# Key pages, scores and sample sums one projection step sooner in a two-layer decoder step, with a fifth buffer for value pages

## What is computed

```python
gq, gk, gv, gg, glr, mu, mv, sq, sk, sv = split_cols(a @ w_in)    # 1024 -> 3088 columns
o_gla, s_gla = gla_mixer(gq, gk, gv, gg, glr, ...)                # gated linear attention, 4 heads
o_gm, v_gm = gmlp_mixer(mu, mv, ...)                              # spatial gating, 4 heads
# stick-breaking attention, 8 heads; the samples see 1024 past keys in 8 pages of 128 rows
z = einsum('bthd,bshd->bhts', q, k) * HEAD_DIM ** -0.5 + bias
log1m = where(mask, -softplus(z), 0.0)
suffix = cumsum(log1m, axis=3, reverse=True) - log1m
A = where(mask, exp(log_sigmoid(z) + suffix), 0.0)
o_sb = einsum('bhts,bshd->bthd', A, v)
o = concatenate([o_gla, o_gm, o_sb], -1) @ w_out
```

## Time and profile before

| | |
|---|---|
| runs of the kernel before | 1373.92, 1377.28, 1377.60 us; median 1377.28 |
| the profiled execution | 1376.02 us, span 1374.3 us |
| TensorE busy | 1319.7 us, 96% of the span; mean granted clock 0.991 |
| VectorE, ScalarE, GpSimd busy | 795.0, 585.0 and 81.6 us |
| moved | 324.59 MB, mean 236 GB/s |
| last input projection step ends (first layer) | 384.67 us |
| last `new_values` ends (first layer) | 443.43 us |

### The profile page before, as it was taken

The page is one execution under the profiler, slowest core; times in us unless marked ns, Lnnn a source line. Parts: engine busy times, 40 slices in busy tenths (PEclk is TensorE's granted clock), DMA queues, the critical chain, the costliest instruction groups (busy, mean ns, idle before and its releaser), DMA issues.

```text
span 1374.3 us, 34322 instructions
## 1 busy us (share of the span) xinstructions
PE 1319.7 (96%) x13994; PEld 1261.9 (92%) x13994; DVE 795.0 (58%) x1160; ACT 585.0 (43%) x963; POOL 81.6 (6%) x158
## 2 busy tenths in 40 slices
PE   6899999999989999999999999998998998999998
PEld 5899999999976899999989999998997787999998
DVE  2554554567895655555465555446788657555544
ACT  2533333443465543334453333345346555333343
POOL 4000000010041000000000000002003100000000
PEclk9899999999999999999999999999999999999999
DMA  9878789789989895568875566996998993565453
GB/s 329 252 229 270 214 249 307 220 257 325 313 269 355 259 325 153 154 168 277 269 237 154 161 174 199 293 269 192 334 336 251 331 325 106 160 175 155 138 168 98
DMA packets 424008, 324.59 MB, mean 236 GB/s; under 512 B 15655, under 2 KB 351911, under 8 KB 423888
## 3 DMA queue, kind: packets, MB, share of 16 engines
q1 hardware_dynamic: 421124, 317.03, 75.9%
q0 software_dynamic: 2464, 5.71, 1.3%
q10 hardware_dynamic: 300, 0.13, 0.0%
HBM read 318.03 MB, written 4.78 MB: 235 GB/s over the span
## 4 chain that ended last, share of the span: by engine, by line
PE 85%; DVE 4%; DMA 4%; SPq 2%; ACT 2%; issue 1%; DVEq 1%; POOL 0%; ACTq 0%
PE PS L601 23%; PE PS L602 23%; PE PS L603 23%; PE PS L627 4%; PE PS L885 2%; PE PS L655 2%; PE PS L656 1%; PE PS L657 1%; SPq L450 1%; PE PS L931 1%; DMA direct<-in_cache_sb_v 1%; DMA raw<-in_mix_w_out 1%; DMA raw<-in_ffn_w_in 1%; DVE w_lo L1684 1%; DVE direct L1959 1%
## 5 line engine op out<-in xcount | busy, mean ns | idle before, releaser
L1684 DVE TENSOR_TENSOR w_lo<-raw,w_hi 128x1024 fp32r<-128x1024 f32 (+1 forms) x368 | 392.9, 1106 | 443.8 <-ACT w_hi L1298 443.3
L1298 ACT ACTIVATE w_hi<-raw 128x1024 fp32r<-128x1024 f32 (+1 forms) x368 | 337.5, 960 | 651.5 <-PE PS L603 574.6
L601 PE MATMUL PS<-a_hi,w_hi 128*128 128x288 f32 x1760 | 524.0, 298 | 0.8 <-ACT ysq L1656 0.6
L602 PE MATMUL PS<-a_lo,w_hi 128*128 128x288 f32 x1760 | 519.2, 295 | 0.0
L603 PE MATMUL PS<-a_hi,w_lo 128*128 128x288 f32 x1760 | 517.6, 294 | 0.0
L601 PEld LDWEIGHTS PS<-a_hi,w_hi 128*128 128x128 f32 x1760 | 329.8, 187 | 4.7 <-issue 3.8
L603 PEld LDWEIGHTS PS<-a_hi,w_lo 128*128 128x128 f32 x1760 | 331.4, 188 | 0.0
L602 PEld LDWEIGHTS PS<-a_lo,w_hi 128*128 128x128 f32 x1760 | 330.4, 188 | 0.7 <-issue 0.4
L602 PE MATMUL PS<-h_lo,w_hi 128*128 128x288 f32 x704 | 208.4, 296 | 0.0
L601 PE MATMUL PS<-h_hi,w_hi 128*128 128x288 f32 x704 | 208.1, 296 | 0.0
L603 PE MATMUL PS<-h_hi,w_lo 128*128 128x288 f32 x704 | 208.0, 296 | 0.0
(11 more groups left out here) (321 smaller groups left out, 1134.6 us busy)
## 6 DMA issues: line engine op xcount, KB each, us to landing
raw<-in_ffn_w_in SPq DMA_DIRECT2D x176, 512.0 KB, 5.0
direct<-in_cond_w SPq DMA_DIRECT2D x240, 256.0 KB, 5.0
direct<-in_cache_sb_k SPq DMA_DIRECT2D x128, 256.0 KB, 4.6
direct<-in_cache_sb_v SPq DMA_DIRECT2D x128, 256.0 KB, 4.3
raw<-in_ffn_w_out SPq DMA_DIRECT2D x64, 384.0 KB, 3.7
raw<-in_mix_w_in SPq DMA_DIRECT2D x48, 512.0 KB, 7.4
raw<-in_ffn_w_out SPq DMA_DIRECT2D x64, 320.0 KB, 4.3
side<-in_cond_w SPq DMA_DIRECT2D x48, 256.0 KB, 5.3
```

The lines of the kernel that those rows point to most:

```text
L601: pe.matmul(out, whi, hi, start=begins and i == 0, stop=False)
L602: pe.matmul(out, whi, lo, start=False, stop=False)
L1298: act.activation(w_hi[:, s, at_:at_ + n], raw[:, s, at_:at_ + n], ACT.Copy)\
L1684: tt(w_lo[:, s, at_:at_ + n], raw[:, s, at_:at_ + n], w_hi[:, s, at_:at_ + n], ALU.subtract).then_inc(lo_done.sem, 1)
```

## The change

- Key chunks `2j-4` and `2j-3` follow step `j`, from 2 to 9. VectorE turns them at the end of its part of step `j-1`, behind the split; two queries are spread at step 2. SyncE interleaves key chunks with weights accordingly.
- The transpose of the query copies goes between the two halves of step 2, `part_offsets(0)` between those of step 10. The key rows (`rows_of(.., SK, ..)`) go behind step 10 and into step 11, `regroup(0)` directly behind step 11 with its result in banks 4 to 7.
- The sums of sample group 0 go from VectorE's step 10 to step 8, the offsets and weights to steps 10 and 11. The cap of group 1 moves from GpSimd to VectorE, its sums ahead of the prompt's masks. The gate's SiLU with its two table loads moves from ScalarE's step 11 to step 10.
- A fifth buffer, `extra`, takes value chunks 4, 9 and 14; the others rotate through `direct`. Value chunk 0 comes before the last two `prompt_scores`.
- On ScalarE `values_by_sample` and `prompt_log1p_exp(2)` go behind `weights_by_page(1)` and `sample_rows(0)`; `prompt_log1p_exp(0)` goes ahead of the first `gla_rows`. On TensorE `prompt_sums(1)` goes behind `regroup(1)`, which waits for `prompt_less(0)` alone.
- The weights of output steps 2 and 3 are issued ahead of the conditioning chunks. Tiles of the GLA state move, and the waits that this asks for are added.

```diff
-    KEYS_AT = {j: (2 * j - 6, 2 * j - 5) for j in range(3, 11)}
+    KEYS_AT = {j: (2 * j - 4, 2 * j - 3) for j in range(2, 10)}
...
+        extra = tile("extra", [P, 2048])
+        a_turn0 = tile("a_turn0", [P, 4 * NPG * 32], F32, at[0] - 8192)
...
+            def extra_chunk(l, n):
+
+                found = page_table_entries(4 * n)
+                if n < 5:
+                    sp.wait_ge(a_moved.sem, a_moved.at(l, 1))
+                else:
+                    sp.wait_ge(extra_used.sem, extra_used.at(l, n // 5))
...
-                mix_in(2, 3)
+                mix_in(2)
                 key_chunks(l, 0, 1)
+                mix_in(3)
+                key_chunks(l, 2, 3)
                 mix_in(4)
-                key_chunks(l, 2, 3)
-                mix_in(5)
                 for j in range(3, 9):
-                    mix_in(j + 3)
-                    key_chunks(l, *(n + 4 for n in KEYS_AT[j]))
+                    mix_in(j + 2)
+                    key_chunks(l, 2 * j - 2, 2 * j - 1)
+                mix_in(11)
                 for n in range(NPC):
-                    if n == 4:
+                    if n % 5 == 4:
+                        extra_chunk(l, n)
+                    else:
+                        page_chunk(l, cache_sb_v, DP_V, 4 * n, n - (n + 1) // 5)
+                    if n == 3:
                         for s in range(2):
                             mix(l, mix_w_out, POS_MO, s, s, s * 256)
-                    page_chunk(l, cache_sb_v, DP_V, 4 * n, n, n)
                 for s in range(2):
+                    mix(l, mix_w_out, POS_MO, 2 + s, s, (2 + s) * 256)
                     cond_seam(l, 0, 2 * s, 2 * s + 2)
-                    mix(l, mix_w_out, POS_MO, 2 + s, s, (2 + s) * 256)
...
+                            if (j, h) == (10, 0):
+                                pe.wait_ge(gate_x.sem, gate_x.at(l, 1))
+                                part_offsets(0, 7)
+                            if (j, h) == (11, 0):
+                                pe.wait_ge(z_got.sem, z_got.at(l, 5))
+                                rows_of(2, SK, 5, k_t)
...
+                    if j == 11:
+                        pe.wait_ge(off_added.sem, off_added.at(l, 1))
+                        pe.wait_ge(kv_k.sem, kv_k.at(l, 3))
+                        regroup(0)
...
+                pe.wait_ge(kv_v.sem, kv_v.at(l, 3))
+                turn_new(1)
                 pe.wait_ge(gm_y.sem, gm_y.at(l, 2))
-                prompt_sums(1, 2)
...
-                pe.wait_ge(c_sub.sem, c_sub.at(l, 2))
+                pe.wait_ge(c_sub.sem, c_sub.at(l, 1))
                 regroup(1)
                 new_values(0)
...
+                pe.wait_ge(a_copied.sem, a_copied.at(l, 2))
+                prompt_sums(1, 2)
+                value_chunk(8)
```

More of the change, by code:

```diff
@@ L473, in cond, with page_table_entries @@
                     cond_load(L - 1, c * D - D, slot)
-            def page_chunk(l, cache, dp, first, n, wait):
+            def page_table_entries(first):
                 _, found = nc.values_load_multi_w_load_instructions(
@@ L924, in value_chunk @@
                             pe.wait_ge(o_rows_got.sem, o_rows_got.at(l, g))
[L925 to L928, removed]
+                    d = n - (n + 1) // 5
+                    if n % 5 == 4:
+                        rows, done, by = extra[:, :], extra_used, 1
+                        pe.wait_ge(extra_in.sem, extra_in.at(l, n // 5 + 1) * 64)
+                    else:
+                        rows, done, by = direct[:, d % 4, :], direct_used, 1 if n < NPC - 1 else 4
+                        k = direct_in[d % 4]
+                        pe.wait_ge(k.sem, k.at(l, DP_V // 4 + 1 + d // 4) * 64)
+                    if n == NPC - 1:
+                        for slot in range(1, 4):
+                            pe.sem_inc(direct_in[slot].sem, 64)
                     for t in range(4):
@@ L932, in value_chunk @@
                                              a_keys[:, 4 * half + t, 32 * p:32 * p + 32],
-                                             direct[:, n % 4, 512 * t + p * P:512 * t + p * P + P],
+                                             rows[:, 512 * t + p * P:512 * t + p * P + P],
                                              start=v == 0 and t == 0, stop=False)
-                    last.then_inc(direct_used.sem, 1)
+                    last.then_inc(done.sem, by)
                 def new_values(g):
@@ L951, in turn_rows, with rows_of @@
                     last.then_inc(o_turned.sem, 1)
+                def rows_of(i, f0, bank, done):
+                    sl, n = token_tile(i)
+                    for p in range(PR):
+                        last = pe.transpose(PS[0:n, bank, p * P:p * P + P], Fm[:, f0 + p, sl], ident[:, :])
+                    last.then_inc(done.sem, 1)
                 for j in range(N_MI):
@@ L1048, in prompt_values @@
                     last.then_inc(op_sum.sem, 1)
-                def rows_of(i, f0, bank, done):
-                    sl, n = token_tile(i)
-                    for p in range(PR):
-                        last = pe.transpose(PS[0:n, bank, p * P:p * P + P], Fm[:, f0 + p, sl], ident[:, :])
-                    last.then_inc(done.sem, 1)
                 def gla_rows(i, bank):
@@ L1584, in sample_heads @@
                     last.then_inc(o_headed.sem, 1)
+                weights_by_page(0)
                 act.wait_ge(gate_b.sem, gate_b.at(l, 1))
@@ L1996, in turn_weights @@
                         dve.wait_ge(a_moved.sem, a_moved.at(l, g))
-                    dve.transpose(a_turn[:, :], z[:, g, 0:NZ]).then_inc(a_turned.sem, 1)
+                    else:
+                        dve.wait_ge(direct_used.sem, direct_used.at(l, DP_K + NPC))
+                    dve.transpose((a_turn if g else a_turn0)[:, :], z[:, g, 0:NZ]).then_inc(a_turned.sem, 1)
                 def spread_new(g):
@@ L2321, in _ @@
                 after(off_sum, l, 1)
-                pool.wait_ge(z_got.sem, z_got.at(l, 5))
-                new = z[:, 1, NZ:].rearrange("p (b t) -> p b t", t=TS)
-                pool.tensor_tensor(new, new, new_mask[:, :].unsqueeze(1).to_broadcast([P, 4, TS]), ALU.add)
-                pool.drain()
-                pool.tensor_scalar(sm[1][:, :], z[:, 1, :], TOP_Z, None, ALU.min).then_inc(ss_n.sem, 1)
                 pool.wait_ge(gate_e.sem, gate_e.at(l, 1))
```

206 lines of the change are left out of this document (113 added, 93 removed).

## The result

The change is slower, by a little: 1382.33 us median of 16 runs (1379.03 to 1384.78) against 1377.81 us (1373.72 to 1383.78), a ratio of 1.0032 with a 95% interval of 1.0020 to 1.0043. By the ratio that is 4.4 us, just over what this measurement can tell from no change. A second series of the same kernel gave 1.0039 (1.0022 to 1.0056). The prediction had said 1377.4 us and a range up to 1381.5: the time lies 0.8 us above it.

A forecast was written before the change was run, and what follows sets the result against it. TensorE, 96% busy, was taken as the bound: its own work plus waits. Per layer 0.7 + 0.3 us later, for two layers, less 0.6, gave +1.4 us on 1376.0, so 1377.4 us; range 1370.5 to 1381.5.

The forecast's parts named there:

- The query transpose waits 0.7 to 0.8 us: Between the halves of input step 2, TensorE newly waits 0.7 to 0.8 us for VectorE's query copy.
- Key waits go: In the input projection, TensorE's 0.3 us wait for key chunk 15 disappears.
- prompt_scores(2) waits 0.8, gla_rows(2) 1.7, regroup(1) at 417.0: Between input projection and regroup(1): new waits of 3.0 us in all, yet regroup(1) starts 2.9 us earlier.
- my walk: Hand-following of waits between queues through the first layer, using the earlier trace's instruction times; last input step ends at 387.2.
- Pages no longer bound: Value chunks' waits for pages vanish; chunk 15 is there at 436, six us before its use.
- From regroup(1) to prompt_sums(3) 15.4 us, waits 4.4: ScalarE's queue takes 15.4 us beside 11.0 of TensorE work; TensorE waits 4.4, and prompt_sums(3) starts 2.1 us later.
- The last `new_values` 0.7 us later: At the first layer's mixer end, the last new_values ends at 444.1 instead of 443.43.
- 0.7 + 0.3 - 0.6: Second layer's sum: new_values 0.7 us later, output products' a_lo wait 0.3, output step 3's weight wait 0.6 saved.
- Output step-3 weights earlier, -0.6: Second layer: weights issued ahead of two conditioning chunks save TensorE's 0.6 us wait; the chunks' delay costs nothing.
- my first paragraph: Claimed a change that only moves work can win no more than TensorE's waits: 13.4 us for both mixer layers.
- The rival of the table loads: Each ScalarE table switch costs a drain, 1.9 us more per layer: 1381.2 us; chance 0.05.

The follow-up runs named there:

- its second profile: The change run once more, unchanged, as a control: 1382.19 us (11 runs), 1.0039.
- the kernel with the FFN weights first: The change with the first FFN step's weights (slot 0) issued ahead of conditioning chunks 2 and 3: 1379.30 us, 1.0026.
- The kernel with the GLA copy moved: The change with FFN weights first, values_by_sample and pair 2's logarithm ahead of regroup(1), and ScalarE's first GLA copy ahead of pair 0's logarithm: 1373.31 us, 0.9971.
- the softplus kernel: The kernel with the GLA copy moved, plus pair 2's softplus ahead of the spread of new weights on VectorE: 1382.37 us, 1.0019.
- the five-edit kernel: The change with FFN weights, values_by_sample, pair 2's logarithm, first GLA copy and first mask all issued sooner: 1382.49 us, 1.0051.

## Why the prediction was wrong

Step by step, in the order of the prediction:

- *The query transpose waits 0.7 to 0.8 us*: 0.84. *Key waits go*: they did.
- *prompt_scores(2) waits 0.8, gla_rows(2) 1.7, regroup(1) at 417.0*: 1.5, 1.6, and 418.4. On the clock of before, the last input step ends at 387.0 (387.2 in my walk) and TensorE stands at `prompt_scores(2)` from 391.2 on, as in my walk. The copy that it needs was ready at 392.7 instead of 392.0. So `regroup(1)` comes 1.5 us earlier than before and not 2.9; the gain of this stretch was sized too high.
- *Pages no longer bound*: right, in every variant.
- *From regroup(1) to prompt_sums(3) 15.4 us, waits 4.4*: 16.7 us in the change's profile, with waits of 2.7 and half-clock work in the rest; 15.7 us in its second profile, where this stretch has the full clock, with waits of 4.5. Cause and size were right.
- *The last `new_values` 0.7 us later*: it ends 162.4 us behind the mixer's first product, against 159.3 before: 3.1 us later, and 162.3 in the second profile. How much of that is the clock's can be seen in the second layer of the kernel with the FFN weights first, a mixer at the full clock throughout: 161.0, against 159.3 and 160.0 in the two layers of before, 1.0 to 1.7 us later. In the same layer the mixer's column sums of `yacc` start 0.5 us later than in before's second layer, where my sum has 0.7 + 0.3 - 0.6 = 0.4. With the unforeseen wait mended and the clock full, the sum holds there.
- *Output step-3 weights earlier, -0.6, the conditioning chunks are used 20 us later, in the seam, and cost nothing*: **this step failed.** The 0.6 us came: no product step waits for `ysq` any more. But I asked only who uses the chunks that moved back, and not what is queued behind them on SyncE. There stand the FFN weights, and behind their split on VectorE the sum of squares that ends the mixer. Two runs put it at 2.5 us (each to about 1 us): one mends it in the change, the other makes it in before. With it the sum is +3.9 us; 4.4 were measured, and 2.8 (+-0.8) at the same clock.
- *The clock* has no term in the sum at all. I took the granted clock of the profiled execution (0.991) as given and costed waits at their own length. Nor are the waits all that a change can win or lose, as my first paragraph has it: before's profile holds 25 us of half clock. The change's runs have a clock lower by 0.0031 on average, and at 0.78 us for each 0.001 that goes with 2.4 us. At the same clock the change is 2.8 us slower than before; the two make the 5.2 us between the means of all runs.
- *The rival of the table loads*: the loads at 371.94 and 373.93 take 1.28 us each, and the SiLU between them starts 0.02 us behind the first. What followed the second started 0.73 us behind it, 0.03 us behind the operation of VectorE that it waited for. The Trainium skill ("ScalarE: Activation LUTs", What ACT_TABLE_LOAD costs) has a drain of about 1380 ns on top of each switch; the trace shows none here either.

So the result is on the slower side by two things: the wait that the sum put at nothing, which is settled, and the lower clock, which it left out and which goes with the rest. **What stays open** is why the change has a lower clock. It is not the swap on SyncE (0.9902 with it in before). It is not `values_by_sample` or the FFN weights (0.9857 with either mended, as the change's 0.9858). Whether the row of small products around `regroup(1)` has a part in it was not settled. The kernel with the GLA copy moved has 0.9876 and 46 us of TensorE waits in its profile, the one with the softplus moved as well 0.9811 and 44. The clock does not go by the sum of the waits, and a run's clock is an average over stretches that fall in other places each time; one profile for each kernel does not tell what decides.

## What to carry to other kernels

When a transfer is moved back in a queue because its data are used late, look at what stands behind it in that queue, and then at what stands behind that one's consumer on its engine: both queues are in order, and the loss came two steps from the move. An operation that costs nothing does so in one idle stretch; moved behind a hand-over it gets a price (4.8 us of copies in each layer, 3.9 us of time for both layers), and the group-1 sums show the same from the other side. When two profiles are laid over each other, take as zero the first instruction of the stretch in question. Counted from the seam ahead of the mixer, which has a half-clock stretch in before and none in the change, `regroup(1)` would seem to stand at 417.0. Where TensorE is 96% busy, compare kernels at the same granted clock before giving a difference of a few us to an edit.

## What was not expected of the hardware

**The clock.** TensorE's granted clock fell to half in stretches in which it was busy 10 us out of 10 by the profile, with no wait above 0.6 us in the 10 us before (the softplus kernel at 415). In the change it fell at 415 in one profile and at 400 in the next. Within a kernel, some runs at 0.981 took 8 to 9 us more than some at 0.988 (the kernel with the FFN weights first: 1386.3 us at 0.981 and 0.982, 1378.2 and 1377.1 at 0.988).

**VectorE beside GpSimd.** GpSimd's timeline in the five-edit kernel, and VectorE's scans there:

```profile
389.96 3.61 POOL L2383 TENSOR_TENSOR gt<-gt,Fm 128x576 f32<-128x576 f32 x2 [9.23 <-ACT gt L1642]
```

```profile
370.09 2.44 DVE L2026 TENSOR_TENSOR_SCAN sm<-ones,sm 128x256 f32<-128x256 f32 x4
...
389.94 4.76 DVE L2026 TENSOR_TENSOR_SCAN sm<-ones,sm 128x256 f32<-128x256 f32 x4
...
1060.00 4.77 DVE L2026 TENSOR_TENSOR_SCAN sm<-ones,sm 128x256 f32<-128x256 f32 x4
```

The scans of group 0 at 370 have no GpSimd work beside them; those of group 1 run beside two products of GpSimd. A scan takes 0.68 us by the median and up to 1.84 us there, so each of the two products holds one scan up by 1.2 us. The products take 1.8 us each beside the scans and 1.4 us in the change. The Trainium skill ("SBUF — State Buffer", Who interferes with whom) says that a VectorE instruction with two inputs in SBUF contends with a GpSimd instruction that reads SBUF, and that the lock on the shared ports is exclusive. The trace agrees, 1.84 us against 0.68. The change pays for it too, on a product of VectorE at 389.94 beside GpSimd's products: 1.58 us, against 0.74 in the five-edit kernel, where GpSimd does nothing then. Whoever moves VectorE work in this kernel has to look at what GpSimd does then.
